# First half of the second output projection moved beside the last stick-breaking pair, and the second block's weights split by ScalarE and VectorE

## The reference

```python
proj = modulate(rms_norm(x), shift_mix, scale_mix) @ w_in
oa = chunked_rel_attention(qa, ka, va, rel_bias)      # 8 heads
ob = stick_breaking_attention(qb, kb, vb)             # 8 heads
mixed = concatenate([rms_norm(oa) * g_a, rms_norm(ob) * g_b]) @ w_out
x = x + gate_mix * mixed
h = modulate(rms_norm(x), shift_ffn, scale_ffn)
gate, val = split(causal_depthwise_conv(h @ w_up, conv_w, conv_b))
x = x + gate_ffn * ((silu(gate) * val) @ w_down)
```

## Time and profile before

| | |
|---|---|
| median of 3 runs | 2849.94 us (2849.79 to 2856.61) |
| profiled execution | 2849.96 us, of which 2848.2 us are the span of the trace |
| TensorE busy | 2711.2 us, 95% of the span |
| VectorE, ScalarE, GpSimd busy | 1576.3, 774.8 and 292.6 us |
| mean granted clock of TensorE | 0.948 of full speed |
| chain that ended last | TensorE 88%, VectorE 7% |

### The profile page before, as it was taken

How to read it: one execution, slowest core, us unless ns; L and a number is a source line. 1 busy time by engine, 2 the same in 40 slices (tenths; PEclk the granted TensorE clock), 3 DMA queues, 4 the chain that set the end, 5 groups by cost and what they waited for, 6 DMA issues and landing times.

```text
span 2848.2 us, 33078 instructions
## 1 busy us (share of the span) xinstructions
PE 2711.2 (95%) x12560; PEld 2212.3 (78%) x12560; DVE 1576.3 (55%) x2308; ACT 774.8 (27%) x1337; POOL 292.6 (10%) x134
## 2 busy tenths in 40 slices
PE   8999989999999999989989999997889999999998
PEld 6777868888888887868777777766768888888887
DVE  6667464434444466454333567686657655555566
ACT  2244231111110125453333344435032212111122
POOL 6304200000000000022111212030400000000000
PEclk9986999999999999989999999966999999999999
DMA  3403113232232333130010000001102211111111
GB/s 115 34 6 119 30 52 96 66 98 84 76 88 68 96 109 22 46 106 23 25 33 25 23 16 23 8 30 59 45 1 62 65 49 54 44 44 52 37 52 67
DMA packets 198061, 152.92 MB, mean 54 GB/s; under 512 B 53944, under 2 KB 174272, under 8 KB 197952
## 3 DMA queue, kind: packets, MB, share of 16 engines
q1 hardware_dynamic: 178784, 116.55, 14.4%
q10 hardware_dynamic: 19168, 34.90, 4.7%
HBM read 143.04 MB, written 8.41 MB: 53 GB/s over the span
## 4 chain that ended last, share of the span: by engine, by line
PE 88%; DVE 7%; issue 2%; ACT 2%; DMA 1%; SPq 0%; DVEq 0%; ACTq 0%
PE pd L731 27%; PE pd L732 25%; PE pd L733 25%; PE pt L1302 2%; PE pt L1286 1%; PE pt L731 1%; PE pt L1304 1%; DVE actT_lo L1832 1%; PE pt L929 1%; PE pt L947 1%; DVE tail L2268 1%; PE pt L732 1%; PE pt L733 1%; DVE actT_hi L1831 1%; PE pt L750 1%
## 5 line engine op out<-in xcount | busy, mean ns | idle before, releaser
L731 PE MATMUL pd<-actT_hi,st_hi 128*128 128x512 f32 x1872 | 758.7, 405 | 18.7 <-DVE st_lo L2098 10.2
L733 PE MATMUL pd<-actT_hi,st_lo 128*128 128x512 f32 x1872 | 740.4, 396 | 0.0
L732 PE MATMUL pd<-actT_lo,st_hi 128*128 128x512 f32 x1872 | 740.4, 395 | 0.0
L731 PEld LDWEIGHTS pd<-actT_hi,st_hi 128*128 128x128 f32 x1872 | 357.9, 191 | 99.0 <-issue 11.2
L733 PEld LDWEIGHTS pd<-actT_hi,st_lo 128*128 128x128 f32 x1872 | 358.1, 191 | 77.5
L732 PEld LDWEIGHTS pd<-actT_lo,st_hi 128*128 128x128 f32 x1872 | 358.9, 192 | 68.0
L731 PE MATMUL pd<-mv_hi,hid_hi 128*128 128x512 f32 x864 | 337.0, 390 | 3.5 <-DVE acc L2314 1.5
L732 PE MATMUL pd<-mv_lo,hid_hi 128*128 128x512 f32 x864 | 336.2, 389 | 0.0
L733 PE MATMUL pd<-mv_hi,hid_lo 128*128 128x512 f32 x864 | 336.2, 389 | 0.0
L661 POOL TENSOR_TENSOR st_hi<-raw,ones 128x1024 fp32r<-128x1024 f32 x38 | 94.0, 2474 | 1562.6 <-PE pd L733 1551.0
L1561 ACT ACTIVATE mv_hi<-raw 128x1024 fp32r<-128x1024 f32 x54 | 55.9, 1056 | 614.2 <-PE pd L733 477.9
(11 more groups left out here) (306 smaller groups left out, 4152.9 us busy)
## 6 DMA issues: line engine op xcount, KB each, us to landing
raw<-in_w_ff SPq DMA_DIRECT2D x64, 512.0 KB, 4.0
ada_raw<-in_w_ada ACTq DMA_DIRECT2D x64, 384.0 KB, 3.3
raw<-in_w_up SPq DMA_DIRECT2D x44, 512.0 KB, 3.8
raw<-in_w_in SPq DMA_DIRECT2D x30, 512.0 KB, 3.8
raw<-in_w_down SPq DMA_DIRECT2D x22, 512.0 KB, 3.5
acc<-in_x SPq DMA_DIRECT2D x16, 512.0 KB, 6.1
raw<-in_w_out SPq DMA_DIRECT2D x12, 512.0 KB, 3.5
raw<-in_w_ple_gate SPq DMA_DIRECT2D x8, 512.0 KB, 4.0
```

Of the source, the lines that this page charges most:

```text
L731: pe.matmul(out_ap, a_hi, b_hi, start=start, stop=False, skip_group_check=check)
L732: pe.matmul(out_ap, a_hi, b_lo, start=False, stop=False, skip_group_check=check)
L733: return pe.matmul(out_ap, a_lo, b_hi, start=False, stop=stop, skip_group_check=check)
```

## The change

1. `out2`, c = 0: its eight row tiles become sixteen half tiles of 12 matmuls (`first_half_row`), placed in TensorE's counts 77 to 92, beside pair 3. `oa` is turned as it is, in counts 73 to 76 (`turn_mixed`); the factors g go into the weights (`mix_weight_hi`, `mix_weight_lo`), and one over the root mean square of a row is applied when a tile leaves (`first_half_sum` on VectorE, counts 78 to 93). The squares of `oa` run beside pair 0 on ScalarE, and their inverse roots are computed by 14 small operations on VectorE at count 16. The gate diagonals are made at count 71. `x_mid`, the saved rows, is loaded into `rows3` by SyncE after the outputs of step 71.
2. `out2`, c = 1: blocks of `ob` for rows 0 to 511 are turned in counts 93 to 96, the others between row tiles 9 and 10. Roots of `ob` are taken while tiles 8 and 9 run.
3. The norm and the turning for the up projection (`m2`) begin inside c = 1 and go on inside the first two tiles of the up projection (`early_turns`, `first_tiles`), as the first block does it.
4. All weight units after `ffa`'s second are split by ScalarE and VectorE, those of the second in-projection right behind the q, k and v jobs (`in2_hi`, `in2_lo`). GpSimd does nothing after the first two units of `ffa`.

```diff
+            def first_half_row(n):
+                r, h = n // 2, n % 2
+                if n == 0:
+                    pe.wait_ge(w_ready, UN["out2"] + 4)
+                    pe.wait_ge(tp_lo, TPJ["o2"] + 8)
+                if n >= 2:
+                    pe.wait_ge(c0_free, n - 1)
+                for j in range(4):
+                    last = passes(pd[:, 0, h * HB:(h + 1) * HB], actT_hi[:, j, r * P:(r + 1) * P],
...
+                last.then_inc(c0_done, 1)
...
+                elif 73 <= s < 77:
+                    for b in range(2 * (s - 73), 2 * (s - 72)):
+                        if b < 2:
+                            pe.wait_ge(gb_rows, 1)
+                        else:
+                            pe.wait_ge(tp_lo, TPJ["o2"] + b - 1)
+                        turn_mixed(b, pd[:, 0, b % 2 * HB:(b % 2 + 1) * HB])
+                elif 77 <= s < 93:
+                    first_half_row(s - 77)
...
             pe.wait_ge(o_rows, 16)
...
-            pe.wait_ge(gb_rows, 2)
-            norm_transposes("o2", 8)
-            pe.wait_ge(tp_lo, TPJ["o2"] + 8)
-            out_chunks(CH["out2"], UN["out2"], actT_hi, actT_lo, None, TILE["upa"],
-                       lambda: pe.wait_ge(tp_lo, TPJ["o2"] + 16))
-            norm_transposes("m2", 16, rows3, (0,))
+            for b in range(12, 16):
...
+            spread_gate(8, pt[:, 0:2, :].rearrange("p a b -> p (a b)"))
+            second_row(2)
+            second_row(3)
...
+            for r in range(4, RT):
+                second_row(r)
+                early_turns("m2", r)
...
-            tile(0, 0, UN["upa"], 0, T_UP, 8 * CH["ups"],
-                 turned("m2", lambda: norm_transposes("m2", 16, rows3, (1,))))
+            first_tiles("m2", UN["upa"], CH["out2"] + 1)
...
+            def first_half_sum(n):
+                r, h = n // 2, n % 2
+                c = slice(h * HB, (h + 1) * HB)
+                dve.wait_ge(c0_done, n + 1)
+                if n == 0:
+                    dve.wait_ge(mid_in, 16)
+                dve.scalar_tensor_tensor(out=half_gated[:, h, :], in0=pd[:, 0, c], scalar=rsq_a[:, r:r + 1],
+                                         in1=mix_gate[:, c], op0=ALU.mult, op1=ALU.mult).then_inc(c0_free, 1)
```

More of the change, by code:

```diff
@@ L463, in unit_of, with in2_unit, block_of, next_in2 @@
                     val(seg["units"], UN[name] + c + 1))
+        def in2_unit(i, u):
+            slot, at = (UN["in2a"] + u) % 2, (TILE["in2a"] + u + 1) % 2
+            hi, lo = (w_[:, at, 0:8, :].rearrange("p k n -> p (k n)") for w_ in (st_hi, st_lo))
+            landed = i * 48 + (SEG["in2a"]["rows"][u % 6][2] + u // 6 * 48)
+            return hi, lo, raw[:, slot, 0:D], (raw_in[slot], landed), i * 6 + (UN["in2a"] + u + 1)
+        def block_of(name, n):
+            return (n + 4) % 8 if name == "m2" else n % 8
+        def next_in2(q, e):
+            u = ({3: 3, 5: 4} if q == "alone" else {1: 3 * q + 2, 3: 3 * q + 3, 5: 3 * q + 4}).get(e)
+            return u if u is not None and u < 24 else None
         block = ctx.enter_context(nc.Block())
@@ L744, in transposes, with turn_job @@
                         last.then_inc(tp_done, 1)
[L746 to L747 removed]
+            def turn_job(name, half, n):
+                job, src = TPJ[name] + 8 * half + n, rows3 if name == "m2" else acc
+                kt = block_of(name, n)
                 pe.wait_ge(tp_lo, job - 3)
@@ L1306, in outputs3, with spread_gate, turn_mixed @@
                 last.then_inc(b_pv, 1)
+            def spread_gate(n0, bank):
+                for n in range(8):
+                    last = pe.matmul(bank[:, n * P:(n + 1) * P], ones[:, :], diag[:, n0 + n, :], start=True, stop=True)
+                last.then_inc(bc_mm, 1)
+            def turn_mixed(b, bank):
+                if b < 8:
+                    half, src = b // 4, rows2[:, :, b % 4 * P:(b % 4 + 1) * P]
+                else:
+                    half, src = b // 4 - 2, rows2[:, :, HB + b % 4 * P:HB + (b % 4 + 1) * P]
+                for r in range(4):
+                    last = pe.transpose(bank[:, r * P:(r + 1) * P], src[:, 4 * half + r, :], ident[:, :])
+                last.then_inc(tp_done, 1)
@@ L1336, in up_chunk @@
                 per = 0 if i is None else 8
-                for j in range(1, 2 * nh + (not last)):
+                for j in range(2 if name == "ups" else 1, 2 * nh + (not last)):
                     chunk_tile(name, at, j, per, nh, first, 8 * CH[name] - 2 + j if j < 3 else None)
```

450 lines of the change are left out of this document (300 added, 150 removed).

## The result

The changed kernel takes 2803.45 us, the median of four runs (2799.57 to 2812.31), against 2849.86: a ratio of 0.9841, 95% interval 0.9808 to 0.9875. A second set of five runs gave 0.983 (0.9805 to 0.9854). It is faster by 46 us; the forecast was 67 us faster, and the time lies just at the upper end of the range, 2804 (the second set's median, 2808.74, lies above it).

The account below looks back on a forecast made before the run. TensorE, busy 95%, was taken to be slow at a low clock or idle around the turn. Terms -56 + 13.5 - 15.6 - 3 - 2.6 - 3.5 = -67.2 took 2849.96 us to 2783 us, range 2765 to 2804.

Parts of the forecast that it names:

- The weights of the second in-projection: Splitting them on ScalarE and VectorE in the attention pairs, mostly hidden by TensorE: -3 us, bounds -12 and +8.
- Counts 70 to 77: Pair 3's start: scan of step 72 at 1871.2, count 73 2.7 us, four counts of 3.4, half tile 0 at 1887.5.
- Counts 77 to 92: Half tiles beside pair 3: TensorE bounds steps of 4.9 us, 78 us plus 3 for a low clock, ending at 1968.5.
- Counts 93 to 96 and the end: End of pair 3: VectorE takes 19.1 us, the last outputs 3.4; tile 8 then starts at 1991, -56 us so far.
- Tile 8 to 15: Row tiles of `out2`, c = 1: 57.0 us against 43.5, with a new 3.6 us wait for tile 11; +13.5 us.
- Behind it: From tile 15 to the second up tile's exit, turning inside the first tiles: 34.2 us instead of 49.8, -15.6.
- `ffa` and ahead of the in-projection: Operations no longer slowed by GpSimd's splits: -3.5 us in `ffa`, -2.6 us ahead of the in-projection.
- The rule weighed: Turned blocks in counts 73 to 76 leave the clock low, costing 3 us; by the rows possibly 0, sum -70.2.
- handoffs as the bound: Rival: VectorE's handoffs, not TensorE's matmuls, set the half-tile steps beside pair 3: 6.2 us each, 2804 us; chance 0.10.
- The low clock through pair 3: Rival: clock stays low beside the half tiles, 2853 us, or through the projection too, 2890 us; chance 0.03 each.

Follow-up runs that it names:

- Experiments 1: Changed kernel with the 15 second in-projection weights split during the chunked attention given back to GpSimd: 2791.68 us, ratio 0.9782 to the kernel before.
- 2: Changed kernel with the third weight split of each chunked pair moved to the head of the next pair: 2796.97 us, ratio 0.9804 to the kernel before.
- 3: Changed kernel with VectorE's weight rests in the chunked pairs moved from ahead of the next maximum to behind it: 2786.32 us, ratio 0.9754.
- Experiment 11: As experiment 10, plus TensorE turning the step's own probabilities ahead of the spread diagonals at count 72: 2773.34 us, ratio 0.9731.
- experiment 10: Changed kernel with chunked rests behind the maximum, diagonals built early, bank-freeing adds ahead of side work, and row 1's sum first: 2775.29 us, ratio 0.9716.
- Experiment 8: Changed kernel with half the first projection's inner dimension left out, 6 matmuls per half tile instead of 12: 2794.23 us, ratio 0.9809.
- experiment 5: Changed kernel with VectorE's add that frees an output bank put ahead of its count's side work: 2805.01 us, ratio 0.9828.
- experiment 12: As experiment 11, with the step's own turning ahead of the side work in counts 72 to 76: 2768.01 us, ratio 0.9706.

## Why the prediction was wrong

The direction and the main gain were right: what bounded the kernel was the turn and the low clock, and both went. The size was 21 us off: two terms of the sum were mis-sized, 15 us in the first and 8 in the second. Step by step, as the prediction put it:

- **"The weights of the second in-projection ... I take -3"**: this step failed. It measured +12.4, beyond its bound of +8: -7.3 in pairs 0 to 2 and +19.7 in the chunked pairs. (That the -7.3 come from VectorE's operations beside GpSimd's splits is argued; no experiment takes it apart.) The prediction counted VectorE's 1.25 us as work that TensorE hides. It did not ask what stands behind it in VectorE's queue: the maximum, then exponential, turning, `pT_lo`, and at the end of this chain TensorE, which waits there for `pT_lo` 0.95 us already. Nor did it price the clock behind such a wait. Experiments 1, 2 and 3 show it, and 3 gives the sign back: 321.4 - 323.1 = -1.7, with -7.3 that is -9 for the term.
- **Counts 70 to 77**: the scan of step 72 came 15.3 us after that of 69, predicted 15.6. From it to half tile 0 it took 24.2 us, predicted 16.3. This second step failed, and makes the whole miss of the start of tile 8. The four blocks' counts of 3.4 us took 4.2 (1880.99 to 1897.75), inside their bounds; count 73, for which 2.7 stood, took 6.9: VectorE waited 2.91 us for the copy of the step's own turning, which stood behind the spread on TensorE, and 1.26 for a weight. The prediction had added up VectorE's own operations and no wait in that count. Experiment 11 shows that the turning's place alone is 1.0 us of it; the spread, the gate copy and the weight behind it hold the rest. With the turning first in count 72, and then in 72 to 76, the way from the scan of step 72 to half tile 0 is 19.1 and 17.4 us, where experiment 10 has 23.8.
- **Counts 77 to 92**: half tile 0 to the end of half tile 15, 1898.33 to 1979.2, is 80.9 us, predicted 81. Experiment 8 confirms the bound. That `half_gated` and `mid_in` would not stop TensorE held too. But that the sum is met to 0.1 us is luck in part: the 80.9 hold a wait of 2.47 us for a freeing add, which was not foreseen, and experiment 5, where 0.96 us of it are left, is 3 to 4 us shorter, so that the term of 78 us was some 3 us too large.
- **Counts 93 to 96 and the end**: 23.0 us to the start of tile 8, predicted 22.5. Tile 8 started at 2002.21, against "near 1982": the 20 us are the two failed steps.
- **Tile 8 to 15**: +15.3, predicted +13.5; the new wait ahead of tile 11 was 3.45 us, predicted 3.6, and came where it was said. **Behind it**: -16.7, predicted -15.6; with the third up tile -19.1, 3.5 better than predicted.
- **`ffa` and ahead of the in-projection**: -3.6 instead of -6.1. TensorE's wait fell from 10.08 to 5.88 us, but not all of it moved the end.
- **The rule weighed**: the sum took 3 us for a low clock in the half tiles, the rows said possibly none. It was at 0.50 until about 1903: half tile 0 took 5.2 us (1898.33 to 1903.53), 2.5 more than 12 x 0.227. By the Trainium skill (TensorE: Matmul & The Clock Gate, Part 4: PE-mode transpose) turned blocks do not bring the full clock. The changed kernel agrees: turned blocks and short matmuls ran at 0.50 from 1886 to 1898, and it rose within the dense matmuls of half tile 0. The earlier trace rows disagree. In experiment 12 the same blocks ran and the clock stood at 1.00 among and behind them (1854 to 1878). The runs leave open what lets it rise.
- **The rivals**: handoffs as the bound is out (experiment 8); that its time, 2804, is close to the measured one is chance. The low clock through pair 3 did not come: 0.96 and 0.98 from 1910 to 1970.

## What to carry to other kernels

When work goes to a faster engine's queue, its duration is the small part of the price. Ask which instruction it stands in front of, and how far the chain from there reaches an engine that is waiting already; then look for the gap in that queue where it costs nothing (here behind the maximum instead of ahead of it: 21 us for twelve operations of 1.23 us). Where another engine waits for a step's own handoff, side work on a shared engine belongs behind it, not ahead of it (between experiments 10 and 12, 23.8 us became 17.4 by that order alone). And compare executions by stretches between landmarks where a stage that was not touched varies as much as the effect.

## What the runs showed of the hardware

- With the same instructions, the last exponential of the first attention came at 254.01 in one execution and at 262.20 in another. The granted clock from 110 to 140 us was 1.00 in the first and 0.60 in the second; towards the end it was 0.50 in both (225 to 254, and 225 to 262). These 8.2 us are most of the 10.8 between the two executions (2801.4 and 2812.2).
- At the end of a chunked pair one TensorE wait of 2.05 us was followed by some 10 us at 0.50 in which TensorE had no gap; waits of 0.95 and 0.62 us at the same place by some 3.5 us.
- In 1898 to 1902, while the saved rows arrived at 418 GB/s, the half tile's matmuls were no slower than the clock explains (steps of 0.42 to 0.43 us at 0.50, as in the earlier trace rows).
